# Spreading the second block's head-norm and y-norm roots: one fp32r product over 128 rows in place of one fp32 product over 20 or 8 rows

## The reference, cut to what matters

```
def rms_norm_2(x, g):
    xf = x.astype(jnp.float32)
    xf = xf * lax.rsqrt(jnp.mean(xf * xf, axis=-1, keepdims=True) + EPS)
    return (xf * g.astype(jnp.float32)).astype(x.dtype)
...
    q = rotary(rms_norm_2(q, q_norm_g), pos)
    k = rotary(rms_norm_2(k, k_norm_g), pos)
...
    y = y.reshape(bsz, L, D_INNER) * jax.nn.silu(z)
    y = rms_norm_2(y.reshape(bsz, L, SSD_GROUPS, D_INNER // SSD_GROUPS),
                 norm_g.reshape(SSD_GROUPS, D_INNER // SSD_GROUPS))
```

## Time and profile before

| | us |
|---|---|
| median of 3 executions | 3062.33 (3062.26 to 3063.79) |
| profiled execution, its own time | 3059.11 |
| its span, first to last instruction | 3057.8 |
| TensorE busy with products | 2984.6 (98%) |
| VectorE busy | 1839.7 (60%) |
| ScalarE busy | 1472.9 (48%) |
| GpSimd busy | 1104.8 (36%) |
| share of TensorE in the chain that ended last | 86% |

### The profile page before, as it was taken

The page is one execution under the profiler, slowest core; times in us unless marked ns, Lnnn a source line. Parts: engine busy times, 40 slices in busy tenths (PEclk is TensorE's granted clock), DMA queues, the critical chain, the costliest instruction groups (busy, mean ns, idle before and its releaser), DMA issues.

```text
span 3057.8 us, 49521 instructions
## 1 busy us (share of the span) xinstructions
PE 2984.6 (98%) x20284; PEld 2617.8 (86%) x20284; DVE 1839.7 (60%) x3265; ACT 1472.9 (48%) x2497; POOL 1104.8 (36%) x446
## 2 busy tenths in 40 slices
PE   7999999999999998999999999999999999999999
PEld 5888887877788886799999977888999978889999
DVE  2777775566676546577465555764465466664654
ACT  3453333454433325655465446664355456654553
POOL 0422322000322231245455432444545523435554
PEclk9999999999999999999999999999999999999999
DMA  7546652211366742178455432434555433335554
GB/s 254 200 157 195 199 193 88 78 56 42 124 206 234 250 133 74 42 258 271 128 165 182 147 118 83 125 111 138 171 161 178 146 111 105 111 117 166 170 189 138
DMA packets 404560, 459.90 MB, mean 150 GB/s; under 512 B 8688, under 2 KB 381424, under 8 KB 404336
## 3 DMA queue, kind: packets, MB, share of 16 engines
q1 hardware_dynamic: 401248, 453.32, 46.1%
q10 hardware_dynamic: 3088, 3.42, 0.4%
HBM read 455.66 MB, written 1.05 MB: 149 GB/s over the span
## 4 chain that ended last, share of the span: by engine, by line
PE 86%; DVE 6%; ACT 4%; POOL 2%; issue 1%; DMA 1%; ACTq 0%; DVEq 0%
PE bank L445 24%; PE bank L447 23%; PE bank L446 23%; POOL wl L420 1%; PE banks L445 1%; PE banks L447 1%; PE banks L446 1%; ACT wh L386 1%; PE bank L1456 1%; DVE wl L405 1%; PE bank L649 1%; PE banks L1467 1%; DMA X<-in_ctxT 1%; PE banks L1804 1%; PE banks L1793 1%
## 5 line engine op out<-in xcount | busy, mean ns | idle before, releaser
L420 POOL TENSOR_TENSOR wl<-raw,wh 128x768 fp32r<-128x768 f32 (+3 forms) x324 | 980.5, 3027 | 1790.7 <-ACT wh L386 1790.7
L386 ACT ACTIVATE wh<-raw 128x2048 fp32r<-128x2048 f32 (+1 forms) x336 | 636.1, 1893 | 460.3 <-PE bank L447 386.9
L405 DVE TENSOR_TENSOR wl<-raw,wh 128x1280 fp32r<-128x1280 f32 (+3 forms) x332 | 496.1, 1494 | 445.5 <-ACT wh L386 445.3
L445 PE MATMUL bank<-nh,wh 128*128 128x272 f32 (+1 forms) x1712 | 505.3, 295 | 3.4 <-DVE nl L2170 2.8
L447 PE MATMUL bank<-nh,wl 128*128 128x272 f32 (+1 forms) x1712 | 493.2, 288 | 0.0
L446 PE MATMUL bank<-nl,wh 128*128 128x272 f32 (+1 forms) x1712 | 491.7, 287 | 0.0
L445 PE MATMUL bank<-xh,wh 128*128 128x512 f32 (+2 forms) x1282 | 440.9, 344 | 4.2 <-DVE xl L783 3.7
L447 PE MATMUL bank<-xh,wl 128*128 128x512 f32 (+2 forms) x1282 | 433.9, 338 | 0.0
L446 PE MATMUL bank<-xl,wh 128*128 128x512 f32 (+2 forms) x1282 | 433.6, 338 | 0.0
L445 PEld LDWEIGHTS bank<-nh,wh 128*128 128x128 f32 x1712 | 325.0, 190 | 31.1 <-issue 23.9
L445 PE MATMUL bank<-hh,wh 128*128 128x512 f32 (+1 forms) x1024 | 344.1, 336 | 0.0
(11 more groups left out here) (476 smaller groups left out, 5611.5 us busy)
## 6 DMA issues: line engine op xcount, KB each, us to landing
raw<-in_mlp_w SPq DMA_DIRECT2D x128, 1024.0 KB, 5.6
raw<-in_w_in SPq DMA_DIRECT2D x60, 1024.0 KB, 5.3
raw<-in_mod_wT SPq DMA_DIRECT2D x48, 1024.0 KB, 5.1
extra<-in_mod_wT SPq DMA_DIRECT2D x36, 1024.0 KB, 5.5
raw<-in_w_mlp_up SPq DMA_DIRECT2D x32, 1024.0 KB, 5.5
raw<-in_w_mlp_down SPq DMA_DIRECT2D x32, 1024.0 KB, 5.1
raw<-in_w_in SPq DMA_DIRECT2D x34, 512.0 KB, 5.1
raw<-in_w_ssd_down SPq DMA_DIRECT2D x16, 1024.0 KB, 5.1
```

The source lines that it names most:

```text
L386: nc.scalar.activation(self.wtile(self.wh, c1), self.rawtile(c1), AF.Copy).then_inc(*up("act_wh", ("wh", c1)))
L405: nc.vector.tensor_tensor(l, r, h.bitcast(F32), ALU.subtract).then_inc(*up("dve_wl", ("wl_dve", c1), *([("wl_pool", c1)] if n == self.P[c1 ...
L420: nc.gpsimd.tensor_tensor(l, r, h.bitcast(F32), ALU.subtract).then_inc(*up("pool_wl", ("wl_pool", c1), *([] if n else [("wl_dve", c1)])))
L445: nc.tensor.matmul(o, ah, bh, start=first, stop=False)
```

## The change

The roots get two parts. After `dve_root` a new function writes their fp32r value to `rsp` rows 0 up, and root minus that value to rows 32 up. `rsp` is 128 x 272, set to zero once in `dve_join`. The spreads become one fp32r product of 128 rows: for the head norms with `spread` as weights, which is now 128 x 1280 in fp32r and copied from `eye`; for the y norm with one column of `eye`, broadcast to 128. The accumulation in TensorE adds the two parts. The spreads wait for `rsp` instead of `rs`. What multiplies, and everything else, is as before.

```
+    def dve_root_parts(self, name, n, T):
+        nc, at, up, DVE = self.nc, self.T.at, self.T.up, self.DVE
+        DVE.wait_ge(*at("rs", name))
+        nc.vector.tensor_copy(self.rsp[0:n, T], self.rs[0:n, T]).then_inc(*up("dve_rsp", ("rsh", name)))
+        DVE.wait_ge(*at("rsh", name))
+        nc.vector.tensor_tensor(self.rsp[32:32 + n, T], self.rs[0:n, T], self.rsp.bitcast(F32)[0:n, T], ALU.subtract).then_inc(*up("dve_rsp", ("rsp", name)))
...
+        self.rsp = put("rsp", LT, F32R)
...
-        self.spread = put("spread", 1280)
+        self.spread = put("spread", 1280, F32R)
...
+        nc.vector.memset(self.rsp.bitcast(F32)[:], 0.0).then_inc(*up("dve_const", ("const2",)))
...
-                    PE.wait_ge(*at("rs", f"h{l}"))
-                    nc.tensor.matmul(b[:, 0:LT], self.spread[0:20, 128 * k:128 * k + 128], self.rs[0:20, 0:LT], start=True, stop=True
+                    PE.wait_ge(*at("rsp", f"h{l}"))
+                    nc.tensor.matmul(b[:, 0:LT], self.spread[:, 128 * k:128 * k + 128], self.rsp[:], start=True, stop=True
...
-        nc.vector.tensor_copy(self.spread[0:20, :].rearrange("p (k c) -> p k c", c=64), self.ident[0:20, 0:20].unsqueeze(2).broadcast_to([20, 20, 64])
+        nc.vector.tensor_copy(self.spread[:].rearrange("p (k c) -> p k c", c=64), self.eye.bitcast(F32)[:, 0:20].unsqueeze(2).broadcast_to([128, 20, 64])
...
         self.dve_root(name, rs, tmp, v)
+        self.dve_root_parts(name, 20, SEQ)
...
-            PE.wait_ge(*at("rs", f"y{l}"))
-            nc.tensor.matmul(b[:, T], self.ident[0:8, g:g + 1].broadcast_to([8, 128]), self.rs[0:8, T], start=True, stop=True
+            PE.wait_ge(*at("rsp", f"y{l}"))
+            nc.tensor.matmul(b[:, T], self.eye[:, g:g + 1].broadcast_to([128, 128]), self.rsp[:, T], start=True, stop=True
...
         self.dve_root(f"y{l}", self.rs[0:8, T], self.rtt[0:8, T], self.rv[0:8, T])
+        self.dve_root_parts(f"y{l}", 8, T)
```

## The result

Eight executions of each kernel on one chip: the change takes 3053.11 us (3048.77 to 3055.97), the kernel before 3064.32 (3058.48 to 3066.77). The ratio is 0.9964, with a 95% interval of 0.9954 to 0.9973: 11.0 us less, 8.3 to 14.1. On another chip it was 3052.32 against 3061.30, ratio 0.9972 (0.9963 to 0.9981), 8.6 us less. Forecast were 3054.4, in 3050 to 3060, and 7.9 us less. The profiled execution took 3053.22, its span is 3051.8, 6.0 less than before's.

What follows compares the result with a forecast made beforehand. TensorE, busy 98% of the span, was taken as the bound. Savings of 4.1 + 2.2 + 0.7 + 1.4 less 0.5 made 7.9 us, so 3054.4 us from the median 3062.33, with an 8-in-10 range of 3050 to 3060.

Steps and rivals of the forecast that it cites:

- Price of a dense pair: Y norm after j = 2 and 3, both layers: four pairs fall from 1.30 to 0.25 us each, 4.1 saved.
- Four-spread places: Y norm after j = 1, both layers: last spread about 0.9 plus VectorE's idle 0.21, 1.1 each, 2.2 us saved.
- The clock at the y norm: Both four-spread places: dense work resumes about 1.1 earlier, so less low clock; 0.7 each, 1.4 us gained.
- Head norms: Ten pairs nearly all hidden behind VectorE: 0.7 us won, 0.5 lost if layer 0's longer wait lowers the clock.
- what follows has slack before VectorE: Layer 0's head norms: the reason a clock fall behind the longer wait was priced at only 0.5 us lost.
- What is added: Eight VectorE root instructions, about 0.8 us a root, the memset and the 128-row copy to `spread`: no time lost.
- The sum: Whole kernel: 4.1 + 2.2 + 0.7 + 1.4 - 0.5 = 7.9 us saved.
- Rival 1: Head norms: new VectorE and GpSimd collisions leave 3.2 us saved, 3059.1, no measurable change; chance 0.27.
- Rival 2: Y norm: clock doesn't fall, or half as long in both layers; 3052 to 3048.5 us; chance 0.12.
- Rival 3: Y norm and head norms: idler engine regains its clock later at four places, 3068.9 us, slower; chance 0.05.
- Rivals 4 and 5: Spreads: product isn't cheap, 3061 to 3063 us, chance 0.03; or all 18 pairs count, 3043, chance 0.03.
- The signs: Profile: 20 and 16 matmuls near 290 ns, starts 0.125 apart, L2342 wait near 2.9, no TensorE wait for `rsp`.

Runs made afterwards that it cites:

- h_only: Kernel before with the new fp32r product in the head norms only, y norm spreads left as fp32 over 8 rows: 3059.80 us, ratio 0.9997.
- parts_only: Kernel before plus VectorE's `rsp` parts, memset and waits, while all spreads still read the fp32 roots over 20 and 8 rows: 3063.63 us, ratio 1.0009.
- hi_rows20: The change, but its fp32r products read only the 20 or 8 rows of high parts, low parts left out: 3054.17 us, ratio 0.9988 to before.
- y_only: Kernel before with the new product for the y norm's eight pairs only, head norms spread as before: 3054.16 us, ratio 0.9980.
- fp32_rows128: The change with the same 128-row operands read as plain fp32, two matmuls a product: 3054.96 us, ratio 0.9982 to the kernel before.
- reorder_y: The change, with the y norm's third and fourth spreads moved behind the two tiles of the next gate chunk: 3048.23 us, ratio 0.9961 to before.
- fill_h: The change plus five unused fp32 products of 256 columns in each layer's long wait of the first rotation products: 3052.34 us, ratio 0.9971 to before.
- best_fill: The change with both reorderings (y-norm spreads later, L2354 earlier) plus six dummy products before the second rotation products: 3045.27 us, ratio 0.9955 to before.
- reorder_y_old: Kernel before, fp32 spreads kept, only the y norm's third and fourth spreads moved behind the next gate chunk's two tiles: 3054.90 us, ratio 0.9982.
- early_q: The change, with VectorE's L2354 of the second head-norm pair moved ahead of the first z gate and split: 3052.73 us, ratio 0.9975 to before.
- best: The change with both reorderings, y-norm spreads later and VectorE's L2354 earlier: 3045.63 us, ratio 0.9955 to the kernel before.

## Why the prediction was right

By its steps, against the place-by-place differences of the two profiled executions.

- **Price of a dense pair, 1.05 saved.** By the distances of starts, measured 1.05 twice in layer 0 and 1.02 twice in layer 1: 4.1 us, as forecast. What the prediction didn't know is that 0.39 of it come from the rows and 0.66 from the type.
- **Four-spread places, 1.1 each.** Right. From the last L447 ahead of the spreads to the first L445 behind them it went from 4.65 to 3.56 in layer 0, 1.09 less, and from 4.65 (2742.98 to 2747.63) to 3.44 (2742.56 to 2746.00) in layer 1, 1.21 less. Together 2.3 instead of 2.2. VectorE's idle 0.21 ahead of its first L2846 is gone: L2922 ends and L2858 follows at once.
- **The clock at the y norm, 0.7 each.** Undersized against the execution before. What is left of the 2.3 and the 3.6 won at these places is 1.2 and 2.4, or 3.6 against 1.4. The prediction took the gain nearer to none, as the waits stay. They stay, at 1.09 and 1.31, and yet the low stretch fell from 6.8 to 3.4 in one layer and to none in the other. But the prediction had taken its 6.8 from one execution, and `h_only` and `parts_only` have 3.4 in both layers with the old spreads. Against them the two places together, waits, spreads and clock, give 3.1, where 2.2 + 1.4 = 3.6 was forecast. What holds in every trace is that layer 1 has no low stretch there with the change and has one with the old spreads in the old order.
- **Head norms, 0.7 won and 0.5 lost.** The mechanism was right, the size not. The wait for L2342's successor grew from 0.80 to 2.70 (forecast 2.9), and layer 1's from 1.17 to 3.10. What failed is the step "what follows has slack before VectorE": by the last rotation product nothing was lost (its start is 1.7 late, 1.9 at the first), but then came 10.2 us at 1.2 GHz instead of 3.4. This lost 2.8 of dense work. Together the head norms are 2.3 worse in the two traces, where 0.2 better was forecast. `hi_rows20`, whose spreads are cheap too and whose waits there have grown to 2.15 and 1.57, had 3.4 us of low clock and took 0.3 less than before from the seam to the `PT` product, so the loss comes with the long stretch and not with the cheap spreads as such. The medians speak milder: `h_only` is 0.9 better, with an interval from 2.1 worse to 4.0 better.
- **What is added, nothing.** Right for TensorE: `parts_only` shows the first rotation product at its old time. But the split behind the roots doesn't only start late, as the prediction has it; it meets GpSimd's and takes 3.02. The copy at 0.83 took the lower of the two prices named.
- **The sum.** 4.1 + 2.3 + 3.6 - 2.3 = 7.7 against 7.9. That the trace comes so near is luck: against the one execution before, y gave 2.3 more than forecast, nearly all by the clock, and the head norms 2.5 less, and both errors are lengths of low stretches, which differ from execution to execution. Firm are the 4.1 of the pairs and the grown waits. The time measured was 11.0 less on one chip and 8.6 on the other. The first interval, 8.3 to 14.1, lies just above 7.9, the second holds it. The time itself, 3053.11, is 1.3 from the forecast, and below the 3056.2 from which the prediction said "faster".
- **Rival 1, collisions of VectorE and GpSimd.** At the rotation products they didn't increase: the one collision moved to the instruction ahead, where L1313 took 2.07 beside L420, so 1.6 were lost as before. Among the splits VectorE lost eight more, four behind the roots and four behind the copies to `spread`, 1.2 to 1.7 us each; at the two head roots the next instruction got as much back. None stood where TensorE waited for it. So the rival's mechanism was there and its price wasn't.
- **Rival 2, no fall of the clock at y.** Its condition came true against the execution before: no fall in layer 1, half as long in layer 0. Its saving, 10.4 to 13.8, holds the 11.0 of the first chip and not the 8.6 of the second; in the traces the head norms took part of it back.
- **Rival 3, slower by the clock.** One of its four places came true, the head norms of layer 0.
- **Rivals 4 and 5.** A pair costs 0.25, and `h_only` shows that ten of the 18 pairs don't count.
- **The signs.** Matmuls, lengths, distances, the wait of 2.9 and the 0.8 a root came out as named, and none of the waits is for `rsp`. One sign of being wrong did show: TensorE's wait for VectorE's L1303 in the head norms grew, from 1.40 to 1.94 in layer 0 and from 1.56 to 2.06 in layer 1. `y_only`, with the old spreads there, has 1.42, so it is the cheap spreads ahead of this wait that lengthen it, as they do the first one. The sign doesn't tell a wrong forecast from a hidden saving, and was badly chosen.

**What stays open** is what makes the 10.2-us stretch behind the head norms of layer 0. The traces of the change, its repetition, `h_only`, `fp32_rows128`, `reorder_y` and `fill_h` have it. `best_fill` has 6.8 us there, the kernel before and `hi_rows20` 3.4. Those of `y_only`, `parts_only`, `reorder_y_old`, `early_q` and `best` have none, though the last two have the same waits of 1.9 and 0.5 just ahead of it. `fill_h` has it without the wait of 2.70, and `hi_rows20` lacks it with one of 2.15, so that wait isn't what it needs. The low stretches of the first block, whose instructions are the same, differ between these executions too, so their times may be what decides. No run tells this apart. Open is also how much of the clock's share at the y norm belongs to the change.

## What to carry to other kernels

Price a small product by the distance of starts in the stream around it, and ask two questions of it: how many matmuls it makes, and on how many rows it lies. Here a pair of 0/1 spreads on 8 rows in fp32 cost five times what it costs on 128 rows in fp32r, and a part of that, 0.39 us, was paid once for each group of few-row products. Such a saving counts only where the engine doesn't wait next, and what is won in front of a wait is best followed by moving the waiting product behind dense work, which won 3 to 4 us on top of the 8.6 here and kept the clock up at the y norm. Before a difference at one place is put down to the change, look at the same place in other executions: here it moved by 1.5 us with nothing changed.

## What the hardware showed that was not expected

- A pair of products over 8 rows in a stream of 128-row products costs 0.38 or 0.39 us more than one over 128 rows, in fp32 and in fp32r alike (1.30 against 0.92, 0.64 against 0.25). In fp32 a single product over 8 rows costs 0.85 and the second of a pair 0.45, so the 0.39 is paid once a group.
- Low-clock stretches differ between executions of one kernel, and with them the time: 3054.90 to 3067.37 for the kernel before. They lasted 3.4, 6.8 or 10.2 us in these traces. Behind waits of 1.09 and 1.31 us with 128-row products it was 3.4 or none; behind waits of 0.54 and 0.98 with 8-row products it was 6.8 in one execution and 3.4 in two others.
- When a split of VectorE and one of GpSimd meet, the one that starts second takes long: VectorE's 3.02 instead of 1.49 when it starts 0.32 behind, GpSimd's 3.15 instead of 2.00 when it starts 0.04 behind.
- Writing 128 rows of fp32r took VectorE 0.83 us for 1280 columns, as long as 20 rows of fp32 (0.82).
